# Two-phase MLP: the first two pairs of activated tiles are stored raw and split on their return

## The reference

```
def sq_relu_mlp(h, w1, w2):
    return jnp.square(jax.nn.relu(h @ w1)) @ w2

f = sq_relu_mlp(rms_norm(h, mlp_pre_g[i]), mlp_w1[i], mlp_w2[i])
h = h + rms_norm(f, mlp_post_g[i])
```

## Time and profile before

| | us |
|---|---|
| median of 3 runs | 3073.54 (3073.14 to 3075.14) |
| the profiled execution, its own time | 3074.86 |
| its span, first to last instruction | 3073.1 |
| PE busy | 3000.0 |
| DVE busy | 2056.7 |
| ACT busy | 1382.9 |
| POOL busy | 731.9 |

### The profile page before, as it was taken

One profiled execution on the slowest core, in us unless ns is written; L12 is line 12 of the kernel. 1 busy time (PEld: TensorE's weight loads), 2 busy tenths in 40 slices (PEclk: granted clock), 3 DMA queues, 4 the chain that ended last, 5 costly groups with the idle time before them and its releaser, 6 DMA issues.

```text
span 3073.1 us, 44859 instructions
## 1 busy us (share of the span) xinstructions
PE 3000.0 (98%) x17070; PEld 2453.1 (80%) x17070; DVE 2056.7 (67%) x2833; ACT 1382.9 (45%) x2556; POOL 731.9 (24%) x706
## 2 busy tenths in 40 slices
PE   8999999999999999999999999999999999999997
PEld 7788888887788788877888788878888778878876
DVE  7275647547888777777555566643854788877777
ACT  4435545346777421134111366644533677751212
POOL 0019300000666533320000022100000056653332
PEclk9999999999999999999999999999999999999999
DMA  3110331003666976522222221213100366697653
GB/s 135 35 49 22 112 121 42 28 35 148 228 243 245 342 267 246 205 96 96 96 95 96 80 76 55 58 50 123 49 28 29 136 237 243 246 333 283 246 203 125
DMA packets 167575, 428.90 MB, mean 140 GB/s; under 512 B 12128, under 2 KB 45168, under 8 KB 165616
## 3 DMA queue, kind: packets, MB, share of 16 engines
q1 hardware_dynamic: 128576, 386.79, 34.5%
q10 hardware_dynamic: 38832, 39.85, 3.8%
HBM read 286.08 MB, written 140.51 MB: 139 GB/s over the span
## 4 chain that ended last, share of the span: by engine, by line
PE 78%; DVE 10%; ACT 4%; issue 3%; DMA 2%; POOL 2%; SPq 0%; ACTq 0%; DVEq 0%; POOLq 0%
PE ps L2960 18%; PE ps L2976 14%; PE ps L3182 10%; PE ps L3183 10%; PE ps L3184 10%; PE ps L3409 2%; DMA hid_store<-staged 2%; PE ps L3339 2%; PE ps L3032 1%; DVE work L1892 1%; DVE work L1908 1%; DVE hres L1923 1%; PE ps L3541 1%; PE ps L3414 1%; PE ps L3299 1%
## 5 line engine op out<-in xcount | busy, mean ns | idle before, releaser
L2960 PE MATMUL ps<-act,whi 128*128 128x512 f32 x2384 | 751.5, 396 | 5.4 <-DVE work L2043 2.7
L2960 PEld LDWEIGHTS ps<-act,whi 128*128 128x128 f32 x2384 | 444.1, 188 | 114.6 <-issue 13.9
L2960 PE MATMUL ps<-act,wlo 128*128 128x512 f32 x1192 | 466.8, 392 | 0.0
L1876 DVE TENSOR_TENSOR wlo<-wraw,whi 128x1024 fp32r<-128x1024 f32 x255 | 319.1, 1253 | 208.7 <-ACT whi L986 175.1
L2976 PE MATMUL ps<-act,whi 128*128 128x512 f32 x1376 | 369.8, 390 | 0.7 <-DVE work L2450 0.7
L2335 DVE TENSOR_TENSOR work<-work,ps 128x512 f32<-128x512 f32 x360 | 241.0, 684 | 141.9 <-PE ps L3184 140.0
L883 POOL TENSOR_TENSOR stagedf<-quads 128x1024 f32<-128x1024 f32 x28 | 74.8, 2670 | 1067.4 <-ACTq L1277 1053.1
L2976 PEld LDWEIGHTS ps<-act,whi 128*128 128x128 f32 x1376 | 258.0, 188 | 56.7 <-issue 1.8
L1336 ACT ACTIVATE whi<-wraw 128x1024 fp32r<-128x1024 f32 x112 | 116.6, 1057 | 414.3 <-POOL wraw L902 350.5
L986 ACT ACTIVATE whi<-wraw 128x1024 fp32r<-128x1024 f32 x148 | 155.8, 1057 | 310.5 <-DMA wraw<-wstream_dram 306.9
L2960 PEld LDWEIGHTS ps<-act,wlo 128*128 128x128 f32 x1192 | 223.8, 188 | 49.4
(11 more groups left out here) (384 smaller groups left out, 6342.8 us busy)
## 6 DMA issues: line engine op xcount, KB each, us to landing
wraw<-wstream_dram SPq DMA_DIRECT2D x260, 512.0 KB, 3.5
hid_store<-staged SPq DMA_DIRECT2D x196, 512.0 KB, 3.5
act<-hid_store SPq DMA_DIRECT2D x42, 1024.0 KB, 11.3
hresr<-hid_store SPq DMA_DIRECT2D x56, 512.0 KB, 11.7
qkvz<-work ACTq DMA_DIRECT2D x32, 512.0 KB, 2.6
work<-qkvz ACTq DMA_DIRECT2D x64, 256.0 KB, 3.2
tx<-hid_store SPq DMA_DIRECT2D x28, 512.0 KB, 7.9
act<-hid_store SPq DMA_DIRECT2D x28, 512.0 KB, 12.1
```

The lines of the kernel that those rows point to most:

```text
L1876: TT(wlo[s][:], wraw[s][:], whi[s][:].bitcast(F32), ALU.subtract).then_inc(w_split, 1)
L2960: last = mm(out_of(u)[:, 0:width], (wlo if hl else whi)[s][:, at:at + P], rhs(kt, xp, e), start=kt == hl == xp == 0, stop=kt == kts - 1 an ...
```

## The change

For hp 0 and 1 (`RAW = 2`) nothing is split in the up phase: `part_hi` and `part_lo` return at once, and SP stores the quadrants themselves and POOL's raw sums, 256 KB for each operand of one hp, with waits on the squares and POOL's sums instead of on the splits. When group 0 of the down phase loads its operands (hp 0 and 1), they come as raw float32, 512 KB for both hp in one transfer, into the place of the lo part; ACT copies them to the place of the hi part (`raw_hi`) and DVE subtracts in place (`raw_lo`), 128x1024 each, seven of both. PE's products a1 ... a4 of group 0 wait for DVE's count of these splits, one by one, instead of for landings. ACT gets two waits for the landing of hp 0's stores, ahead of `first_up(4)` and of `first_up(6)`. The orders of `sum_hi("T3")` on ACT and `sum_lo("T3")` on DVE move ahead of the first pair's weight splits. On SP the weight load `n + 2` moves ahead of the loads of T3 and B22.

SP:

```
+                def store_raw(hp, *ops):
+                    at = HIDDEN * layer + hp
+                    for op in ops:
+                        if op in B_AT:
+                            sp.wait_ge(squared, 4 * at + layer + ("B22", "B11", "B21").index(op) + 2)
+                        else:
+                            sp.wait_ge(t_raw, 3 * at + {"T1": 1, "T3": 1, "T2": 2, "T4": 3}[op])
+                        src = quad(hp, op[1:]) if op in B_AT else stage_part(op, 1, True)
+                        sp.dma_start(hid_store[0, STAGED.index(op), :, hp, 0], src).then_inc(out_of_op(op), 16)
+
+                def operand_raw(op):
+
+                    sp.wait_ge(unit_done, up_unit(layer, PAIRS - 1, PRODUCT_OF[op]) + 1)
+                    sp.wait_ge(*all_out(op, layer, RAW))
+                    k, step = RAW_OPS[op]
+                    sp.dma_start(moving(op, 1, 0, 2).bitcast(F32), hid_store[0, STAGED.index(op), :, :, 0, :])                         .then_inc(ops_in[k][step], 16)
...
-                    store(hp, "B11", "B22", "B21", "T1", "T3", "T2", "T4")
+                    store_raw(hp, "B22", "B11", "T1", "T3", "B21", "T2", "T4")
...
-                operand(0, "B11")
-                operand(0, "T1")
+                operand_raw("B11")
+                operand_raw("T1")
                 store(PAIRS, "B21", "T1", "T3", "T2", "T4")
-                operand(0, "B21")
-                operand(0, "T2")
-                operand(0, "T3")
-                operand(0, "B22")
+                operand_raw("T2")
+                operand_raw("B21")
                 load(n + 2)
+                operand_raw("T3")
+                operand_raw("B22")
                 store(PAIRS + 1, "B11", "B22")
-                operand(0, "T4")
+                operand_raw("T4")
                 load(n + 3)
                 store(PAIRS + 1, "B21", "T1", "T3", "T2", "T4")
```

ACT:

```
                 def part_hi(hp, op):
 
-                    if hp == 0 and op == "B11":
+                    if hp < RAW:
+                        return
+                    if hp == RAW and op == "B11":
                         eng.wait_ge(first_out, 32 * (layer + 1))
-                    if hp:
-                        eng.wait_ge(*all_out(op, layer, hp))
+                    eng.wait_ge(*all_out(op, layer, hp))
...
                 first_up(2)
-                part_hi(0, "B11")
-                part_hi(0, "B22")
                 sum_hi("T2")
                 first_up(3)
-                part_hi(0, "B21")
-                part_hi(0, "T13")
-                part_hi(0, "T2")
+                eng.wait_ge(*all_out("B11", layer, 1))
                 first_up(4)
-                part_hi(0, "T4")
                 first_up(5)
+                sum_hi("T3")
                 block_hi(blocks_of(layer, 0)[0])
                 block_hi(blocks_of(layer, 0)[1], prep_no(layer, 0))
                 sums_hi(prep_no(layer, 0), sums_of(0))
-                sum_hi("T3")
+                eng.wait_ge(*all_out("B21", layer, 1))
                 first_up(6)
                 sum_hi("T4")
-                part_hi(1, "B11")
-                part_hi(1, "B22")
+
+                def raw_hi(op):
+
+                    k, step = RAW_OPS[op]
+                    eng.wait_ge(*landed(layer, -k, step))
+                    A(moving(op, 0, 0, 2), moving(op, 1, 0, 2).bitcast(F32), ACT.Copy).then_inc(xt_act, 1)
+
...
                     else:
+                        raw_hi("B11")
+                        raw_hi("T1")
                         down_hi(0, 0)
...
+                raw_hi("B21")
                 last_corner(PAIRS - 1)
-                for op in LO_ORDER[2:]:
-                    part_hi(PAIRS + 1, op)
+                raw_hi("T2")
+                part_hi(PAIRS + 1, "B21")
+                raw_hi("B22")
+                part_hi(PAIRS + 1, "T13")
+                raw_hi("T3")
+                part_hi(PAIRS + 1, "T2")
+                raw_hi("T4")
+                part_hi(PAIRS + 1, "T4")
```

DVE (`part_lo` returns for hp < RAW too):

```
                 sum_lo("T1")
-                part_lo(0, "B11")
-                part_lo(0, "B22")
                 sum_lo("T2")
-                for op in LO_ORDER[2:]:
-                    part_lo(0, op)
+                sum_lo("T3")
                 for n in blocks_of(layer, 0):
                     block_lo(n, prep_no(layer, 0))
                 sums_lo(prep_no(layer, 0), sums_of(0))
-                sum_lo("T3")
                 sum_lo("T4")
-                part_lo(1, "B11")
-                part_lo(1, "B22")
+
+                def raw_lo(op):
+
+                    nth = ("B11", "T1", "B21", "T2", "B22", "T3", "T4").index(op)
+                    eng.wait_ge(xt_act, XT_ACT * layer + 24 + nth + 1)
+                    TT(moving(op, 1, 0, 2), moving(op, 1, 0, 2).bitcast(F32), moving(op, 0, 0, 2).bitcast(F32), ALU.subtract)                         .then_inc(xt_dve, 1)
+
                 for q in range(PAIRS):
...
                     for op in LO_ORDER[2:]:
                         part_lo(q + 1, op)
+                    if not more:
+                        raw_lo("B11")
                     corner(q, "2", "11")
                     if more:
                         block_lo(blocks_of(layer, q + 1)[0], x)
+                    else:
+                        raw_lo("T1")
                     corner(q, "7", "22")
...
                 for i in range(MLP_G - 1):
+                    if i == 0:
+                        raw_lo("B21")
+                        raw_lo("T2")
                     eng.wait_ge(evac, down_unit(layer, i, "a1"))
                     for k in range(len(PRODUCTS)):
                         add(i, k)
                         if i == 0 and k < 4:
                             part_lo(PAIRS + 1, LO_ORDER[2 + k])
+                            if k:
+                                raw_lo(("B22", "T3", "T4")[k - 1])
```

PE, in the down phase:

```
                         if j == 0:
-                            nth = (MLP_G - i % 2) // 2 * layer + i // 2 + 1
-                            if p in "1267":
-                                step = "1267".index(p)
-                                eng.wait_ge(ops_in[i % 2][step], 16 * (3, 1, 3, 4)[step] * nth)
+                            if i == 0 and p in "1526374":
+                                eng.wait_ge(xt_dve, XT_DVE * layer + 16 + "1526374".index(p) + 1)
+                            if i and p in "1267":
+                                eng.wait_ge(*landed(layer, i, "1267".index(p)))
```

More of the change, by code:

```diff
@@ L51 @@
 OPS_STEP = {"B11": 0, "T1": 0, "B21": 1, "T2": 2, "B22": 2, "T3": 3, "T4": 3}
-HIDS = 2 * MLP_T + len(LO_ORDER) * (MLP_T // 2 * (MLP_G - 1))
+RAW = 2
+HIDS = 2 * MLP_T + len(LO_ORDER) * (MLP_T // 2 * (MLP_G - 1) - RAW)
+RAW_OPS = {"B11": (0, 0), "T1": (1, 0), "T2": (0, 2), "B21": (0, 1), "T3": (0, 3), "B22": (1, 2), "T4": (1, 3)}
+PRODUCT_OF = {"B11": "1", "T1": "5", "T2": "6", "B21": "2", "T3": "7", "B22": "3", "T4": "4"}
+XT_ACT, XT_DVE = 24 + len(RAW_OPS), 16 + len(RAW_OPS)
 FIRST_UP = ((0, 1), (1, 1), (0, 0), (1, 0), (2, 1), (3, 1), (2, 0), (3, 0))
@@ L559, in all_out, with hid_no, landed @@
             return out_of_op(op), 16 * (len(EARLY) if op in EARLY else len(STAGED) - len(EARLY)) * (HIDDEN * layer + hp)
+        def hid_no(layer, hp, op=None):
+            return HIDS * layer + 2 * MLP_T + len(LO_ORDER) * (hp - RAW) + (LO_ORDER.index(op) + 1 if op else 0)
+        def landed(layer, i, step):
+            raw = sum(at == (i % 2, step) for at in RAW_OPS.values())
+            each = (3, 1, 3, 4)[step]
+            return ops_in[i % 2][step], 16 * ((raw + 3 * each) * layer + raw + each * ((i + 1) // 2))
         T_AT = {"T1": (0, 0), "T3": (0, 1), "T2": (4, 1), "T4": (4, 0)}
@@ L731, in store @@
                         nth = LO_ORDER.index(op if op not in ("T1", "T3") else "T13")
-                        sp.wait_ge(hid_ready, HIDS * layer + 2 * MLP_T + len(LO_ORDER) * hp + nth + 1)
+                        sp.wait_ge(hid_ready, hid_no(layer, hp) + nth + 1)
                         sp.dma_start(hid_store[hp // 2, STAGED.index(op), :, hp % 2], stage(op).bitcast(F32)).then_inc(out_of_op(op), 16)
+                def store_raw(hp, *ops):
[12 more added lines that the diff above has]
+                    sp.dma_start(moving(op, 1, 0, 2).bitcast(F32), hid_store[0, STAGED.index(op), :, :, 0, :])                         .then_inc(ops_in[k][step], 16)
                 def operand(i, op):
-                    name = {"B11": "1", "T1": "5", "T2": "6", "B21": "2", "T3": "7", "B22": "3", "T4": "4"}[op]
+                    name = PRODUCT_OF[op]
                     used = up_unit(layer, PAIRS - 1, name) if i < 2 else down_unit(layer, i - 2, "d" + name)
@@ L741, in operand @@
                     src, k = hid_store[i, STAGED.index(op)], 2 * (i % 2)
-                    landed = ops_in[i % 2][OPS_STEP[op]]
+                    arrived = ops_in[i % 2][OPS_STEP[op]]
                     if op in B_AT:
                         first, e = B_AT[op]
```

(21 more changed lines are left out.)

4 lines of the change are left out of this document (2 added, 2 removed).

## The result

| | us |
|---|---|
| changed kernel, median of 19 runs | 3079.95 (3073.86 to 3084.64) |
| kernel before, median of 19 runs beside them | 3074.49 (3067.6 to 3077.9) |
| ratio | 1.0019, 95% interval 1.0012 to 1.0026 |
| profiled execution of the changed kernel | 3080.86, span 3079.0, mean clock 0.991 |

The forecast was 3067.0 with a range of 3059 to 3077. The change costs 5.5 us instead of saving 6.4. By the bound of 0.2% it is just "same", at the slow edge, and its interval reaches past it.

The account below looks back on a forecast made before the run. TensorE was taken to bound the kernel; per layer, -4.7 us in the up phase and +1.5 at the down start gave -6.4 us in two layers. From 3074.86 that is 3068.5, 3067.0 as a median, range 3059 to 3077.

Parts of the forecast that it names:

- What bounds it: Whole kernel: TensorE is busy 3000.0 of 3073.1 us, so the change affects only its idle time and clock.
- the up phase: Up phase, q=0: stops at products "6" and "4" and the half clock behind them go, -4.7 us per layer.
- Rival 4: Up phase: ACT's two new waits stop PE in place of the old stops; total 3074.5, chance 0.08.
- What goes at the down start: Down phase, group 0: weights and last stores land sooner, so PE's stop at c7 goes, -4.2 us per layer.
- DVE's order: Down phase, group 0: DVE's queued splits delay the add of a6, so a7 starts at 1055.7, not 1051.64; +4.1 us.
- 0.6 x 7 + 1.14 x 2 + 2.1: Down phase, group 0: DVE's PSUM reads, raw splits and weight split before a6's add ends, 8.6 us.
- The group 0 term: Down start: +4.1 at a7, +1.6 for half clock, -4.2 at c7, giving +1.5 us per layer.
- Rival 2: Down start: DVE pays in full, with two half-clock stretches, +5.1 us per layer; total about 3074, chance 0.20.
- my case: Whole kernel: the main forecast, -4.7 and +1.5 us per layer, 3067.0, reaching from 3063 to 3071; chance 0.45.
- Rival 3: Down start: B21's late landing holds ACT's queue, +6.5 us per layer; total 3080, chance 0.12.
- A total over 3077 would mean that a landing, not DVE's order, sets the down start: Sign of error: a total above 3077 us was to show a load's landing setting the pace of the down start.
- Rival 1: Down start: DVE's turns with POOL cost less, a7 starts at 1051 to 1052; total 3059, chance 0.15.

Follow-up runs that it names:

- e11: Changed kernel with POOL's weight sum for j = 3 of group 0 also waiting for the add of a6; 3078.18 us, one execution.
- e8: e7 with DVE's weight split for j = 0 of the next group one add later, behind d1's; 3059.95 us (5 runs), ratio 0.9955.
- e1: Changed kernel with DVE's seven raw subtractions cut to 8 of 512 columns, every wait kept; 3067.38 us, once.
- e9: Changed kernel with DVE's weight split for j = 2 moved behind the add of b6 in group 1 alone; 3075.48 us, one execution.
- e10: Changed kernel with SP issuing group 1's weight block for j = 2 ahead of group 2's loads of B11 and T1; 3070.79 us, one execution.
- e7: e3 with two waits added on POOL, delaying hp 13's hidden sums and group 0's j = 2 weight sums; 3060.72 us (5 runs), ratio 0.9950.
- e3: Changed kernel with DVE's raw split of T4 moved behind a6's add and the j = 2 weight split behind a7's; 3064.02 us (7 runs), ratio 0.9971.

## Why the prediction was wrong

- **What bounds it, and the up phase: right.** The stops at "6" and "4" and the half clock behind them went, 4.83 and 4.79 us against 4.7. ACT's two new waits cost PE nothing. Rival 4 is out.
- **What goes at the down start: right, and incomplete.** The c7 stop went. The weight block for j = 2, issued at 1026.78, landed 7.6 us later, 2.4 us after a1 (forecast 1.5), and the last stores let POOL go 6.9 us sooner (6). But those landings were counted as a gain only.
- **DVE's order: right in kind.** Counted from a1 (1031.94 here, 1032.53 in the prediction's rows), the split of B21 is done at 8.3 us (forecast 7.8) and that of B22 at 14.5 (14.6); a2's stop is 2.67 (2.2). From there to the end of the add of a6 I had 8.6 us and it took 9.6. The failed term is "0.6 x 7 + 1.14 x 2 + 2.1": the 2.1 for the weight split was 3.1, since POOL's sum for j = 3 came forward onto it. With that sum held a7 is at 23.1 (e11), and the layout's figure was 23.2. The turns in the sum were those of POOL's old timetable; the change moved POOL.
- **The group 0 term, "+1.5 us per layer", was mis-sized**: +3.6 and +4.0. Of the difference 1.0 is that a7, some 1.2 and 0.9 a new stop at d6 (idle 1.01 and 0.77), behind the next group's weight split (1.75 + 2.10 us in turns with POOL), which no step of mine looked at; e8 removes it. The rest is half clock, 1.5 us behind a7 in layer 0 and 2.1 in layer 1 against 1.6.
- **A term was missing from the sum**: group 1, +1.4 and +4.1. I took the c7 stop as 4.2 us won. It had been cover: while PE stood at c7, SP's queue, which is tied to a4, ran on and had group 1's weight block in time. Without the stop a4 to the end of group 0 is 25 us instead of 28, POOL's sum is still 33 us behind a4, and the split is late. That is why e1 missed: it takes the same 25 us from a4 to the end of group 0 (24.7 and 24.9), and its POOL sum is 33.6 behind a4. Two separate edits remove it (e9 on DVE, e10 on SP).
- **The rivals.** Rival 2 had a7 at 25.2 and two half-clock stretches; the truth in group 0 lies between it and my case. Rival 3 has the right total for the wrong reason: B21's load was issued at 1025.43 and took 7.6 us, so that it landed inside the 1031.5 to 1034 that I estimated, and ACT began its copy at 1033.18. The 1 MB load of B21 in the kernel before took 11.6. The sentence "A total over 3077 would mean that a landing, not DVE's order, sets the down start" was wrong. Rival 1 failed: the turns cost all that was charged, and more. The Trainium skill, "SBUF — State Buffer", section "SBUF: two separate sides", has the two engines hold one port pair in turns, an instruction at a time; 4.34 us for two halves beside POOL and 1.02 without it agree.
- **The numbers.** The two layers' sums miss the forecast by 4.1 and 6.5 us; of these 10.6 us, 5.5 are group 1's and 2.1 the stop at d6, terms that the sum did not have at all. The products of the one pair of profiles account for 4.2 of the measured 5.5 us; the other 1.3 is within what single executions scatter, and I leave it open.

## What to carry to other kernels

A stop that a change removes may have been the cover of something later: before counting it as won, follow the chain that ran on during it to the next product that needs it, into the next group if need be. When a change lets one engine start sooner, look for what it now falls on: here POOL, freed early, took DVE's turns where PE waited for DVE, and making it wait was worth some 3 us (e7's sums against e3's, one pair of traces). Of an in-order queue, put behind the instruction that frees the bank whatever is not needed before it; the same raw tiles cost 5 us in one order of DVE and save 6 to 8 in another.

## What the runs showed that was not expected

- The stop of 2.67 us at a2 is followed by half clock in layer 1 and by full clock in layer 0 of the same execution (the rows of 1040.30 and 2732.00 above). It costs nothing there: a3 starts at 14.7 in both layers, since it waits for DVE, and the half clock only shortens its stop (0.39 against 1.94). Here a half-clock stretch was not paid where something else was late behind it.
- At the stop of 6.48 us the half clock lasts 6.8 us, longer than the stretch of the earlier trace rows. But in layer 0, 3.6 of it lie in the stop, and 3.2 us with 8 matmuls remain, where 13.8 would fit: about 1.3 us, no more than behind a short stop. In layer 1 it falls later against the stop: 4.6 us with 11 matmuls remain, where 19.8 would fit, about 2.0 us. I had charged rival 2 a whole second stretch.
- In the profiled pair the stretch from 28.0 to 34.8 has a granted clock of 1.00 before and 0.53 after, in the same part of the program. Most of the 4.2 us between the two executions ahead of layer 0's first pair hangs on such stretches; a few microseconds between single executions say nothing about a change.
